# A hybrid S5/mLSTM/MoE step on one core: gather in 8 passes, S5 products on row and column tiles, w_down in 8 KB rows

## The reference

```
u, q, k, v, o, ig, fg, g_s5, g_ml = split(rmsnorm(x) @ w_in)      # 36 column tiles of 128
bu   = einsum('blgc,gpc->blgp', u, bbar)                          # S5: 32 groups of 16 channels, 64 complex states
h    = complex scan over time of bu
y    = einsum(h_re, c_re) - einsum(h_im, c_im) + d_skip * u
...                                                               # GLU, mLSTM in chunks of 64, gates, w_out
logits = rmsnorm(x) @ w_router + b_router;  top 4 of 32 experts, softmax
per expert e:  gu = x_e @ w_gate_up[e] + b;  h = (clip(up)+1) * (g*sigmoid(1.702 g));  y_e = h @ w_down[e] + b
y = sum over the 4 experts, residual, rmsnorm
```

## Time and profile before

| | us |
|---|---|
| three runs | 1362.22, 1362.23, 1362.48 (median 1362.23) |
| profiled execution | 1362.19 |
| its span, first to last instruction | 1360.4 |
| busy: PE, PEld, DVE, ACT, POOL | 1287.0, 583.1, 499.1, 151.1, 301.3 |
| DMA moved | 440.74 MB |

### The profile page before, as it was taken

How to read it: one execution, slowest core, us unless ns; L and a number is a source line. 1 busy time by engine, 2 the same in 40 slices (tenths; PEclk the granted TensorE clock), 3 DMA queues, 4 the chain that set the end, 5 groups by cost and what they waited for, 6 DMA issues and landing times.

```text
span 1360.4 us, 22425 instructions
## 1 busy us (share of the span) xinstructions
PE 1287.0 (95%) x7804; PEld 583.1 (43%) x7805; DVE 499.1 (37%) x976; ACT 151.1 (11%) x265; POOL 301.3 (22%) x529
## 2 busy tenths in 40 slices
PE   6969999999959999999999999999999999999996
PEld 4645666766743334333334333343333333333332
DVE  3698864533172223222223222232222223222224
ACT  3400111410230000000000000000000000000002
POOL 2828873000042111211111211112111111211100
PEclk9979999999969999999999999999999999999998
DMA  7212212149738999999999999999999999999994
GB/s 209 81 44 71 84 63 93 64 129 318 274 140 345 418 417 417 417 417 417 419 418 418 418 417 417 416 418 418 418 419 417 417 417 417 418 418 418 419 418 184
DMA packets 113504, 440.74 MB, mean 324 GB/s; under 512 B 16100, under 2 KB 45312, under 8 KB 80704
## 3 DMA queue, kind: packets, MB, share of 16 engines
q1 hardware_dynamic: 103136, 437.88, 80.5%
q10 hardware_dynamic: 10336, 2.43, 0.9%
HBM read 437.82 MB, written 1.87 MB: 323 GB/s over the span
## 4 chain that ended last, share of the span: by engine, by line
PE 60%; SPq 20%; DVE 9%; DMA 5%; issue 3%; ACT 2%; ACTq 1%; POOLq 0%; DVEq 0%; POOL 0%
PE psum L749 21%; SPq L346 19%; PE psum L451 13%; PE psum L787 10%; DMA big<-in_w_gate_up_dram 5%; PE psum L729 5%; PE psum L668 3%; PE psum L433 2%; PE psum L527 1%; PE psum L537 1%; DVE m L1558 1%; DVE m L1555 1%; DVE m L1552 1%; ACT m L1025 1%; PE psum L759 1%
## 5 line engine op out<-in xcount | busy, mean ns | idle before, releaser
L749 PE MATMUL psum<-big,m 128*64 128x512 f32 x2048 | 479.2, 599 | 8.7 <-DMA big<-in_w_gate_up_dram 5.0
L1542 DVE TENSOR_TENSOR acc<-acc,psum 128x512 f32<-128x512 f32 (+1 forms) x198 | 126.9, 681 | 593.7 <-PE psum L729 593.6
L749 PEld LDWEIGHTS psum<-big,m 128*64 128x64 f32 x2048 | 134.6, 136 | 319.0 <-issue 239.8
L787 PE MATMUL psum<-big,m 128*64 128x512 f32 x1024 | 226.8, 595 | 0.0
L451 PE MATMUL psum<-big,m 128*128 128x320 f32 x640 | 184.9, 445 | 5.3 <-ACT uT L833 3.5
L1169 POOL COPY m<-uT 96x64 bf16 x32 | 7.5, 233 | 688.3 <-PE psum L773 687.9
L451 PEld LDWEIGHTS psum<-big,m 128*128 128x128 f32 x640 | 122.0, 195 | 60.6 <-issue 14.9
L787 PEld LDWEIGHTS psum<-big,m 128*64 128x64 f32 x1024 | 71.3, 137 | 134.9 <-issue 129.7
L729 PE MATMUL psum<-m 64*128 64x512 f32 (+1 forms) x396 | 110.9, 637 | 3.9 <-DVE acc L1542 2.9
L1025 ACT ACTIVATE m<-m 128x512 f32<-128x512 f32 x32 | 20.2, 631 | 593.3 <-DVE m L1552 593.3
L715 PE MATMUL psum<-m 128*128 128x64 bf16 x2376 | 76.8, 195 | 5.6 <-POOLq L1165 5.6
(11 more groups left out here) (252 smaller groups left out, 894.0 us busy)
## 6 DMA issues: line engine op xcount, KB each, us to landing
big<-in_w_gate_up_dram SPq DMA_DIRECT2D x256, 1024.0 KB, 19.9
big<-in_w_down_dram SPq DMA_DIRECT2D x128, 1024.0 KB, 23.5
m<-in_w_in_dram SPq DMA_DIRECT2D x18, 1024.0 KB, 5.2
m<-in_w_s_glu_dram SPq DMA_DIRECT2D x8, 512.0 KB, 3.9
m<-in_w_out_dram SPq DMA_DIRECT2D x4, 1024.0 KB, 11.3
acc<-in_x_prompt_dram SPq DMA_DIRECT2D x4, 512.0 KB, 5.1
m<-in_w_ml_out_dram SPq DMA_DIRECT2D x2, 1024.0 KB, 4.9
out_dram<-acc SPq DMA_DIRECT2D x2, 512.0 KB, 2.6
```

The lines of the kernel that those rows point to most:

```text
L749: mm = pe.matmul(psum[SLOT * hf:SLOT * hf + SLOT, GB + gu, :], xeT[:, c, :], big[:, base:base + 512], start=(c == 0), stop=(c == GU_CHUNKS ...
L787: mm = pe.matmul(psum[SLOT * hf:SLOT * hf + SLOT, DB, :], hT[:, m, half, :], big[:, base:base + 512], start=False, stop=(c == DN_CHUNKS - ...
L1542: v.tensor_tensor(x, x, psum[0:n, CB + hf, :], ALU.add).then_inc(S("added"), 1)
```

## The change

Five edits, in one kernel:

1. w_down is read so that partition p takes rows 2p and 2p + 1 of a 256-row chunk, 8 KB in one piece, instead of rows p and 128 + p, 4 KB each. `hm` is turned from columns that lie two apart, so that the down products match.
2. In the gather the 64-token tile needs two products instead of three: its top part stands on partitions 0 to 63 and its middle part on 64 to 127 of one matrix. For this its logits, ranks and table rows are made for 128 partitions, the 64 tokens twice. The zeroing of unused rows goes.
3. `s5_in` uses 32 rows for each product instead of 128 (btz is no longer padded with zeros); the imaginary one reads a second copy of u, `uT2`, whose halves are swapped, so that the two lie on different row tiles.
4. `s5_out` is done once for four slices, as eight products with the real ones first, on four column tiles in turn. hh has five buffers.
5. ScalarE writes uT2, and makes three copies of B instead of eight.

```diff
@@ s5 steps in the plan
-            if j >= 2:
-                plan[S5_AT + j].append(("s5_out", j - 2))
+            if j >= 2 and (j - 2) % 4 == 3:
+                plan[S5_AT + j].append(("s5_out", (j - 2) // 4))
@@ expert_chunk, w_down
-                src = a["w_down"][0, bass.ds(e, 1), row:row + 2 * P, :].rearrange("a (k p) n -> p (a k) n", p=P)
-                dst = cut(dst, 2, D)
+                src = a["w_down"][0, bass.ds(e, 1), row:row + 2 * P, :].rearrange("a (p k) n -> p (a k n)", k=2)
@@ TensorE, s5_in and s5_out
-                for k in range(2):
-                    mm = pe.matmul(psum[:, 2 + k, 0:T], btz[:, k, j, :], uT[:, j // 4, :], start=True, stop=True)
+                t = j // 4
+                for k, u in enumerate((uT, uT2)):
+                    s = slice(32 * ((j + 2 * k) % 4), 32 * ((j + 2 * k) % 4) + 32)
+                    mm = pe.matmul(psum[:, 2 + k, 0:T], btz[s, k, t, :], u[s, t, :], start=True, stop=True)
...
-            def s5_out(j):
-
-                q, t = j % 4, j // 4
-                pe.wait_ge(S("h_ready"), j + 1)
-                if q == 0 and t > 0:
+            def s5_out(t):
+
+                pe.wait_ge(S("h_ready"), 4 * t + 4)
+                if t > 0:
                     pe.wait_ge(S("y_read"), t)
                 for k in range(2):
-                    mm = pe.matmul(psum[32 * q:32 * q + 32, 4, 0:T], ctt[:, k, t, 32 * q:32 * q + 32], hh[:, j % 2, k, :],
-                                   start=(k == 0), stop=(k == 1))
+                    for q in range(4):
+                        mm = pe.matmul(psum[32 * q:32 * q + 32, 4, 0:T], ctt[:, k, t, 32 * q:32 * q + 32],
+                                       hh[:, (4 * t + q) % HH, k, :], start=(k == 0), stop=(k == 1), skip_group_check=True)
@@ TensorE, logits and ranks (the same in both)
-                    mm = pe.matmul(psum[0:n, i, 0:NE], xnT[:, k, t0:t0 + n], wrt[:, k, :],
-                                   start=(k == 0), stop=(k == DK - 1))
+                    for at in range(0, P, n):
+                        mm = pe.matmul(psum[at:at + n, i, 0:NE], xnT[:, k, t0:t0 + n], wrt[:, k, :],
+                                       start=(k == 0), stop=(k == DK - 1), skip_group_check=True)
@@ TensorE, gather
+        PARTS = [(q, i, P) for i in range(2) for q in range(3)] + [(0, 2, P), (2, 2, TS)]
...
-                    for i in range(3):
-                        for q in range(3):
-                            mm = pe.matmul(psum[:, XB, k * SLOT:(k + 1) * SLOT], parts[:, q, i, k * P:(k + 1) * P], pb[:, i, :],
-                                           start=(i == 0 and q == 0), stop=(i == 2 and q == 2))
+                    for n, (q, i, rows_) in enumerate(PARTS):
+                        mm = pe.matmul(psum[:, XB, k * SLOT:(k + 1) * SLOT], parts[0:rows_, q, i, k * P:(k + 1) * P], pb[0:rows_, i, :],
+                                       start=(n == 0), stop=(n == len(PARTS) - 1))
@@ TensorE, expert: the transposes of hm
-                        mm = turn(psum[:, (HB, UB)[m // 2], m % 2 * P:(m % 2 + 1) * P], hm[:, m * P:(m + 1) * P], P)
+                        mm = turn(psum[:, (HB, UB)[m // 2], m % 2 * P:(m % 2 + 1) * P], hm[:, m // 2, :, m % 2], P)
@@ ScalarE
                 if j < 4:
+                    act.wait_ge(S("pj_done"), j + 1)
+                    nc.scalar.activation(uT2[64:128, j, :], bank(j)[0:64, 0:T], ACT.Copy).then_inc(S("u2_ready"), 1)
+                    nc.scalar.activation(uT2[0:64, j, :], bank(j)[64:128, 0:T], ACT.Copy).then_inc(S("u2_ready"), 1)
                     evac(j, uT[:, j, :])
...
+                if n < P:
+                    nc.scalar.copy(parts[n:P, 0, i, :], rest[0:n, i, :]).then_inc(S("mid_ready"), 1)
@@ GpSimd, s5_in
-                if j >= 2:
-                    pool.wait_ge(S("y_done"), j - 1)
+                if j >= HH:
+                    pool.wait_ge(S("y_done"), (j - HH) // 4 + 1)
@@ GpSimd: removed
-            nc.gpsimd.memset(btz, 0.0).then_inc(S("btz_zero"), 1)
...
-            for q in range(3):
-                do(nc.gpsimd.memset(parts[64:128, q, 2, :], 0.0))
...
-            do(nc.gpsimd.memset(tab[:, :, :], 0.0))
```

More of the change, by code:

```diff
@@ L55 @@
 TURN = 4
+HH = 5
 assert TURN * CHUNKS % RING == 0 and NE % TURN == 0
@@ L164, in hybrid_stream_step @@
         sn = r.take(NJ, T)
-        btz = r.take(2, NJ, P)
+        btz = r.take(2, 4, P)
+        uT2 = r.take(4, T)
         ctt = r.take(2, 4, P)
@@ L170, in hybrid_stream_step @@
         ptmp = r.take(2, T)
-        hh = r.take(2, 2, T)
+        hh = r.take(HH, 2, T)
         WORK_END = r.at
@@ L702, in _ @@
                     before = cst[0:nb, C_TRI:C_TRI + n] if b == i else ones[0:nb, 0:n]
-                    pe.matmul(psum[0:n, 4, i * NE:(i + 1) * NE], before, msk[0:nb, b, :], start=(b == 0), stop=(b == i))
+                    for at in range(0, P, n):
+                        pe.matmul(psum[at:at + n, 4, i * NE:(i + 1) * NE], before, msk[0:nb, b, :],
+                                  start=(b == 0), stop=(b == i), skip_group_check=True)
             for b in range(3):
@@ L733, in _ @@
             pe.wait_ge(S("parts_ready"), 3)
+            pe.wait_ge(S("mid_ready"), 4)
             pe.wait_ge(S("bias_placed"), 24 * 16)
@@ L863, in b_matrix @@
                 act.wait_ge(S("setup_turned"), SETUP_B)
[L864 to L868, removed]
+                do(nc.scalar.copy(flat(btz[:, 0]), psum[:, 6, :]))
+                do(nc.scalar.copy(flat(btz[64:128, 1]), psum[0:64, 7, :]))
+                do(nc.scalar.copy(flat(btz[0:64, 1]), psum[64:128, 7, :]))
                 act.sem_inc(S("setup_read"), 1)
@@ L937, in _ @@
                 if j == 3:
+                    act.wait_ge(S("u2_ready"), 8)
                     publish(j, "u_ready")
@@ L1014, in _ @@
                 act.wait_ge(S("top_ready"), i + 1)
-                _, t8, _, f8 = (x[0:n] for x in top[i])
+                _, t8, _, f8 = top[i]
                 nc.scalar.activation(f8[:, 4:8], t8[:, 0:4], ACT.Exp, bias=f8[:, 8:9], accum_out=f8[:, 9:10]).then_inc(S("top_exp"), 1)
@@ L1064, in _ @@
             nc.gpsimd.memset(wg, 0.0).then_inc(S("wg_zero"), 1)
-            nc.gpsimd.memset(btz, 0.0).then_inc(S("btz_zero"), 1)
-            nc.gpsimd.memset(bpad, 0.0).then_inc(S("btz_zero"), 1)
+            nc.gpsimd.memset(bpad, 0.0).then_inc(S("bpad_zero"), 1)
             pool.wait_ge(S("cnat_landed"), 32)
@@ L1087, in s5_in @@
                 pool.wait_ge(S("g_ready"), j + 1)
[L1088 to L1089 removed]
+                if j >= HH:
+                    pool.wait_ge(S("y_done"), (j - HH) // 4 + 1)
                 tt = nc.gpsimd.tensor_tensor
                 do.start(tt(ptmp[:, 0, :], Sn, zz[:, b, 1, :], ALU.mult))
[L1092 removed]
+                do.start(tt(hh[:, o, 0, :], C, zz[:, b, 0, :], ALU.mult))
                 do.start(tt(ptmp[:, 1, :], Sn, zz[:, b, 0, :], ALU.mult))
[L1094 to L1096 removed]
+                do(tt(hh[:, o, 1, :], C, zz[:, b, 1, :], ALU.mult))
+                do(tt(hh[:, o, 0, :], hh[:, o, 0, :], ptmp[:, 0, :], ALU.subtract))
+                tt(hh[:, o, 1, :], hh[:, o, 1, :], ptmp[:, 1, :], ALU.add).then_inc(S("h_ready"), 1)
                 pool.wait_ge(S("h_ready"), j + 1)
[L1098 to L1099 removed]
+                nc.gpsimd.tensor_copy(fin[:, 0:2, j], hh[:, o, :, TP - 1]).then_inc(S("fin_ready"), 1)
+                nc.gpsimd.tensor_copy(fin[:, 2:4, j], hh[:, o, :, T - 1]).then_inc(S("fin_ready"), 1)
             def chunk(c):
@@ L1319, in s5_in, with s5_out @@
                 dve.sem_inc(S("g_ready"), 1)
-            def s5_out(j):
-                t = j // 4
-                if j % 4 == 3:
-                    dve.wait_ge(S("y_done"), j + 1)
-                    do(v.scalar_tensor_tensor(out=uT[:, t, :], in0=uT[:, t, :], scalar=vc[:, 8 + t:9 + t], in1=psum[:, 4, 0:T],
-                                              op0=ALU.mult, op1=ALU.add))
-                    dve.sem_inc(S("y_read"), 1)
+            def s5_out(t):
+                dve.wait_ge(S("y_done"), t + 1)
+                do(v.scalar_tensor_tensor(out=uT[:, t, :], in0=uT[:, t, :], scalar=vc[:, 8 + t:9 + t], in1=psum[:, 4, 0:T],
+                                          op0=ALU.mult, op1=ALU.add))
+                dve.sem_inc(S("y_read"), 1)
             def scores(h):
@@ L1468, in of @@
             def of(i):
-                n = TILES[i][1]
-                return [n] + [x[0:n] for x in top[i]]
+                return [P] + list(top[i])
             for group in ((0,), (1, 2)):
@@ L1506, in _ @@
             dve.wait_ge(S("ranks"), 1)
-            dve.wait_ge(S("zeros_set"), 2)
-            for i, (t0, n) in enumerate(TILES):
-                do.start(v.scalar_tensor_tensor(out=tab[0:n, :, i], in0=psum[0:n, 4, i * NE:(i + 1) * NE], scalar=1.0, in1=msk[0:n, i, :],
+            for i in range(3):
+                do.start(v.scalar_tensor_tensor(out=tab[:, :, i], in0=psum[:, 4, i * NE:(i + 1) * NE], scalar=1.0, in1=msk[:, i, :],
```

(4 more changed lines are left out.)

21 lines of the change are left out of this document (7 added, 14 removed).

## The result

The changed kernel takes **1379.7 us** (median of four runs, 1378.34 to 1380.95) against 1362.2 before: a ratio of **1.013**, 95% interval 1.011 to 1.0145. Forecast were 1350.4 us, and a range that ends at 1358. The profiled execution took 1378.34 us.

What follows compares the result with a forecast made beforehand. The weight stream, 30.13 us per expert against TensorE's 28.75, was taken as the bound. Rows -8.4, gather -0.4, S5 -4.5, copies +0.75, ranks +0.7, transposes +0.1 sum to -11.75: 1350.4 us, range 1343 to 1358.

Steps and rivals of the forecast that it cites:

- Gather in 64 products instead of 72: Expert loop: 0.25 us less per expert, hidden by the weight stream; only the first gather counts, -0.4 us.
- Rival 5: Expert loop: strided transposes make TensorE the bound, period 28.5 + x; slower from x = 0.87 us; chance 0.03.
- Rows of w_down: Weight stream: 8 KB rows land at gate/up pace, 0.29 us less for each of 29 experts, -8.4 us.
- estimate of 3.4 us: Weight stream: by the skill's cycles per packet, 8 KB rows gain 1.1% on w_down, about 3.4 us.
- Rival 1: Weight stream: down rows gain only a fixed price per packet, -3.4 instead of -8.4, 1355.4 us; chance 0.15.
- Rival 4: Weight stream: new rows land no faster, S5 gives as forecast, 1358.8 us; chance 0.04.
- S5: S5 stage: steps 7.1 us apart at GpSimd's pace, 6.0 us gained, 1.5 lost to low clock, sum -4.5.
- +1.5: End of S5: TensorE's wait for GpSimd drops its clock; the last of the four losses is uncovered, +1.5 us.
- estimate of 8 us for the step: S5 stage: by the shared SBUF port, VectorE stretches GpSimd's step towards 8 us and nothing is gained.
- price of the copies on ScalarE: Ahead of S5: the second copy of u delays TensorE's third tile and the cosine tables, +0.75 us.
- Rival 2: S5 gains nothing: GpSimd's pace is today's 7.4 or the low clock is paid four times, 1355 us; chance 0.15.
- Rival 3: S5: TensorE's full saving comes through, -22.9 instead of -4.5, 1332 us; chance 0.05.

Runs made afterwards that it cites:

- kernel on 128 rows: Changed kernel with the eighth matmul of each gather group on 128 rows, zeros below the 64, so all 64 have one shape: 1348.6 us.
- 96 rows: Changed kernel with the eighth matmul of each gather group on 96 rows, zeros in the 32 below the 64: 1352.1 us.
- 64 columns: Changed kernel with all gather rows at 128 and the eighth matmul of each group split in two of 64 output columns: 1385.4 us.
- filled wait: Kernel on 128 rows plus 11 matmuls that nobody reads, in TensorE's wait for the first gather's input: 1347.8 us.
- every second group reversed: Changed kernel with every second gather group in reverse order, so 64-row matmuls meet and 4 pairs of shape changes remain, not 8: 1356.3 us.
- 4 KB rows: Kernel on 128 rows with its w_down rows back at 4 KB and the transposes on adjacent columns: 1357.5 us.
- 64-row ones last: Changed kernel with the eight 64-row gather matmuls moved to the gather's end, one after another: 1348.4 us.

## Why the prediction was wrong, point by point

**The step that failed** is *Gather in 64 products instead of 72*: "2.27 us for 72 at full clock, so 8 fewer give 0.25 per expert. It is hidden in the steady state by the stream." I took the count of products and the mean of one of them, and did not look at what the removed zeros had done: they kept all products at one shape. The gather became 1.34 us longer instead of 0.25 shorter, and TensorE's period became 29.88. The 28.5 that I had set for it was wrong as well: the transposes wait for VectorE behind the gather, so a shorter gather takes nothing off the period, and the kernel on 128 rows has 450.04 - 421.22 = 28.82.

29.88 is above the stream's period, 29.84 by my working and 29.82 as measured, so TensorE began with its lead of 16 chunks and never used it up. But the comparison that prices the loss is another. While the lead lasts, TensorE's period counts in full, and before the change the loop averaged 29.26 per expert (906.93 / 31). 31 x (29.88 - 29.26) is 19 us.

**A sign of the price stood in my own rows.** Sixteen chunk products take 3.43 us behind other 128-row ones. Behind a combine on 64 rows they take 3.65, of which 0.07 is the tail of the last (the chain has 3.58 there). The same products are 0.15 us dearer behind other shapes; with the experiments in hand I read this as the change of shape, though these rows alone don't show it. I had the earlier trace rows in hand for what 64-row tiles cost, and read in it only what they save. The rule on changes of the tiling mode (the Trainium skill, TensorEngine Tiling (Array Packing), "Key Properties") bears on this kernel more than either of the two that I weighed.

**Rival 5 had the right place and the wrong cause.** "TensorE becomes the bound of the expert loop", with a period of 28.5 + x. Over the 28.75 of before, the transposes brought 0.08 and the gather 1.05, so x = 1.38 with my 28.5. My own formula then gives 31 x 29.88 - 906.93 = 19.4 us, less 3.4 gained ahead: 1362.2 + 16.0 = 1378.2, where the profiled run took 1378.3. The closeness is in part luck: chunk 5 of expert 0 came 4.0 us earlier (413.00 + 1.83 = 414.83 against 418.87), not 3.4, and what follows chunk 5 of the last expert took 35.4 us, not 34.6. I gave it 0.03 since "nothing in the trace shows a load that expensive", and asked that only of the transposes.

**Rows of w_down: right.** -8.4 forecast, -7.9 and -8.8 measured. In the kernel on 128 rows, chunk 1 to the next chunk 1 takes 1301.20 - 1271.38 = 29.82 us (29.84 said), chunk 7 to chunk 1 1301.20 - 1286.30 = 14.90 (14.9 said). The estimate of 3.4 us, by the Trainium skill (DMA: Bandwidth & Descriptors, "Why small descriptors are slow"), is too low here: at its 1.1% the ratio of the run with the rows alone would be 0.9975, just outside the interval (0.9923 to 0.9964). Rivals 1 and 4 are out with it. In the changed kernel itself this gain doesn't reach the time, since TensorE sets the period.

**S5: the size right, the reason half wrong.** GpSimd's steps and the last output products, changed kernel:

```profile
99.08 0.86 POOL L1101 TENSOR_TENSOR big<-big 128x320 f32<-128x320 f32 x1 [23.58 <-DVEq L1324]
106.03 0.86 POOL L1101 TENSOR_TENSOR big<-big 128x320 f32<-128x320 f32 x1 [0.28 <-DVEq L1324]
204.14 0.86 POOL L1101 TENSOR_TENSOR big<-big 128x320 f32<-128x320 f32 x1 [0.28 <-DVEq L1324]
```
```profile
125.83 2.36 PE L542 MATMUL psum<-big 128*32 128x320 f32 x16 [2.39 <-POOL big L1106]
209.38 1.28 PE L542 MATMUL psum<-big 128*32 128x320 f32 x16 [1.74 <-POOL big L1106]
```
```profile
106.46 0.47 DVE L1310 TENSOR_TENSOR big<-big,psum 128x320 f32<-128x320 f32 x1
113.40 0.47 DVE L1310 TENSOR_TENSOR big<-big,psum 128x320 f32<-128x320 f32 x1
```

Most steps are 6.95 us apart, and the mean of the fifteen is (204.14 - 99.08) / 15 = 7.00 (7.1 said). The last starts at 204.14 (204.0), the output products at 209.38 (209.7). The low-clock stretch is not where I had put it: the first output products run slow (2.36 in place of 1.28), where GpSimd's pace covers it, and the last ones, which I had priced at +1.5, run at 1.28. And the pace has another owner. GpSimd waits 0.28 for VectorE ahead of most steps, while VectorE goes from step to step with about 0.2 us between at most (and one wait of 1.2 us for TensorE in the stage), 6.94 apart: VectorE sets this pace, not GpSimd.

By the shared port of the Trainium skill (SBUF — State Buffer, "SBUF: two separate sides") I had an estimate of 8 us for the step, and no gain; neither came.

The price of the copies on ScalarE was too low. The first step is 1.57 late, not 0.75, and the delay is there in full where the copies first bite, at TensorE's third tile (29.86 against the 28.29 of the earlier trace rows):

```profile
29.86 6.12 PE L454 MATMUL psum<-big,m 128*128 128x320 f32 x16 [6.48 <-ACT uT L841]
```

That is one run of each kernel. The first step starts at 98.7 to 100.6 us in the other traces with this edit and at 97.5 to 99.5 in those without, so the copies' price is known to about a microsecond. Alone, the part gives 5.2 where -4.5 + 0.75 was said. Rivals 2 and 3 are out.

**Gather and router alone: nothing (0.2 us against), as said** (-0.4 and +0.7). Hiding a shorter gather was right: with 0.23 us less on TensorE the transposes only wait longer.

**The clock behind the S5 stage.** The "+1.5" of the prediction comes in some runs and not in others. Below, the last output products, the tile behind them and the window, first in the kernel on 128 rows, then in that with 96. The last row is from the kernel with the S5 part alone:

```profile
209.12 1.28 PE L542 MATMUL psum<-big 128*32 128x320 f32 x16 [1.77 <-POOL big L1106]
210.33 4.57 PE L454 MATMUL psum<-big,m 128*128 128x320 f32 x16
```
```profile
210.87 2.36 PE L542 MATMUL psum<-big 128*32 128x320 f32 x16 [3.35 <-POOL big L1106]
213.17 6.36 PE L454 MATMUL psum<-big,m 128*128 128x320 f32 x16
...
209.00:214.00 5.00, 3.13 (x18) 1.24 (x19) 0.55 (x1) 0.00 (x0) 2.58 (x5) 0.60 0.00 0
```
```profile
209.84 1.28 PE L541 MATMUL psum<-big 128*32 128x320 f32 x16 [3.36 <-POOL big L1101]
```

In the second, TensorE waited 3.35 us, the granted clock of the window is 0.60 where the first has 1.00, and the two groups cost 2.9 us more. The wait alone doesn't decide it, as the last row shows. The nine traces with the S5 edit:

| kernels | wait, us | output products, us | tile behind, us |
|---|---|---|---|
| changed kernel, 128 rows, 64 columns, filled wait | 1.74 to 1.77 | 1.28 | 4.57 to 4.58 |
| 96 rows, every second group reversed, 4 KB rows | 3.34 to 3.37 | 2.36 | 6.30 to 6.36 |
| 64-row ones last | 3.27 | 1.30 | 6.20 |
| S5 alone | 3.36 | 1.28 | 4.57 |

With 96 rows the output matrices then start 4.8 us later than in the kernel on 128 rows (330.03 against 325.26). 2.9 of it is the lower clock, and 1.7 was there at the first S5 step (100.46 against 98.72). At expert 1 it is 2.7 us behind (434.35 against 431.62), since the other kernel had its first products at the lower clock (5.69 against 3.65), but its span ends up 4.5 us longer. The run with half the pairs has the same late start (329.98), and its first gather and first products are slow on top: expert 1 starts 6.2 us later than on 128 rows (437.82 against 431.62), most of the 8.2 us between the two spans. The kernel before, timed beside it, took 1364.3 us, about 2 more than beside the others. Whether the changed kernel's own spread, 2.6 us where the kernel before had 0.4, is of this kind stays open: its other runs have no trace.

## What to carry to other kernels

Before a matmul is made smaller, look at its neighbours: a change between 128 and 64 rows or columns costs about 0.2 us there and back, as much as seven bf16 matmuls of 64 columns, and zeros that keep the shape cost nothing to be seen here. If small shapes can't be avoided, put them side by side. And when two resources are within 5% of each other (28.75 and 30.13 us here), price every edit on the one that "has room" as closely as on the bound. Its room was not the 1.4 us between the two periods. The loop began with a lead of 16 chunks and averaged 29.26 per expert, so TensorE had 0.5 us, and an edit entered as a saving used 1.05. The best version here is the change with zeros kept below the 64 rows: 1348.6 us, 1.0% under the kernel before.

## What the runs showed of the hardware

- A change of TensorE's shape from 128 to 64 rows and back: 0.196 us a pair (8 pairs), 0.21 (4 pairs), lost about evenly on the way in and the way back; from 128 to 64 columns and back 0.19 to 0.21, by the count it is set against; from 128 to 96 rows: none to be seen (2.07 against 2.04 us for 64 matmuls).
- 64-row bf16 matmuls next to each other are no dearer than 128-row ones: eight in 0.40 us, 0.03 apart.
- Rows of 8 KB instead of 4 KB in a third of a stream at 418 GB/s: 0.31 us less in 30.13, 3.0% on the transfers changed.
- In the S5 stage TensorE ran its last output products at the full clock behind waits of 1.74 to 1.77 us in four traces. Behind waits of 3.27 to 3.37 us it fell to the lower level in four traces, for them or for the tile behind them (granted clock 0.60 over 5 us in one of them) and stayed at the full one in a fifth.
